# The down projection with its activations standing and its weights moving, in a two-block transformer kernel on one core

## What is computed

```python
def conv_glu_ffn(h, w_gate, w_up, conv_w, conv_b, w_down):
    S = h.shape[1]
    g = h @ w_gate
    gp = jnp.pad(g, ((0, 0), (CONV_WIDTH - 1, 0), (0, 0)))
    gc = conv_b
    for j in range(CONV_WIDTH):
        gc = gc + conv_w[j] * gp[:, j:j + S]
    return (jax.nn.silu(gc) * (h @ w_up)) @ w_down
...
        x = x + jnp.concatenate([y_pool, y_mla, y_mem], axis=-1) @ w_o[l]
        x = x + conv_glu_ffn(rms_norm(x, g_ffn[l]), w_gate[l], w_up[l], conv_w[l], conv_b[l], w_down[l])
```

## Time and profile before

| | |
|---|---|
| median of three runs | 1657.52 us (1654.44 to 1659.46) |
| profiled execution: span | 1662.7 us |
| profiled execution: time beside its span | the profile has none |
| TensorE busy | 1599.2 us, 96% of the span |
| TensorE weight loads | 1454.6 us, 87% |
| VectorE, ScalarE, GpSimd busy | 1163.1, 872.5, 133.3 us |
| mean granted TensorE clock | 0.989 |
| first and last matmul of the down projection start at | 1408.48 and 1658.65 us |

### The profile page before, as it was taken

One profiled execution on the slowest core, in us unless ns is written; L12 is line 12 of the kernel. 1 busy time (PEld: TensorE's weight loads), 2 busy tenths in 40 slices (PEclk: granted clock), 3 DMA queues, 4 the chain that ended last, 5 costly groups with the idle time before them and its releaser, 6 DMA issues.

```text
span 1662.7 us, 26531 instructions
## 1 busy us (share of the span) xinstructions
PE 1599.2 (96%) x10666; PEld 1454.6 (87%) x10666; DVE 1163.1 (70%) x1742; ACT 872.5 (52%) x1360; POOL 133.3 (8%) x151
## 2 busy tenths in 40 slices
PE   6799999988999999898999999999999999999999
PEld 5587789978999999887789888888888888999999
DVE  4777877977668876656677777777777767555553
ACT  5755546667655455554556445444444444444442
POOL 0000000321120220031414000000000000000000
PEclk9999999999999999998999999999999999999999
DMA  8889985533456864342234455555455455555552
GB/s 350 322 311 363 362 319 203 199 99 129 159 197 254 306 240 169 128 153 76 102 127 158 174 200 178 181 200 188 170 199 193 170 195 195 184 180 199 200 185 77
DMA packets 49131, 332.23 MB, mean 200 GB/s; under 512 B 5424, under 2 KB 8880, under 8 KB 9584
## 3 DMA queue, kind: packets, MB, share of 16 engines
q1 hardware_dynamic: 48640, 328.17, 54.1%
q0 software_dynamic: 368, 2.36, 0.4%
HBM read 328.41 MB, written 2.10 MB: 199 GB/s over the span
## 4 chain that ended last, share of the span: by engine, by line
PE 71%; DVE 12%; ACT 8%; issue 4%; DMA 3%; POOL 2%; ACTq 0%; SPq 0%; DVEq 0%; POOLq 0%
PE ps L1085 20%; PE ps L1081 11%; PE ps L1083 10%; PE ps L1082 10%; PE ps L1086 10%; DVE wl L1753 4%; ACT wh L1371 3%; DVE raw L1789 3%; DMA raw<-in_wts 2%; PE ps L1128 2%; PE ps L1129 2%; PE ps L1130 2%; PE ps L1240 1%; PE ps L1207 1%; DVE hA L2173 0%
## 5 line engine op out<-in xcount | busy, mean ns | idle before, releaser
L1753 DVE TENSOR_TENSOR wl<-raw,wh 128x1024 fp32r<-128x1024 f32 x512 | 623.7, 1232 | 356.5 <-ACT wh L1371 355.8
L1371 ACT ACTIVATE wh<-raw 128x1024 fp32r<-128x1024 f32 x512 | 530.5, 1054 | 369.8 <-PE ps L1083 237.0
L1085 PE MATMUL ps<-hA,wh 128*128 128x512 f32 x1408 | 499.2, 400 | 0.0
L1086 PE MATMUL ps<-hA,wl 128*128 128x256 f32 x1408 | 396.2, 281 | 0.0
L1081 PE MATMUL ps<-hB,wh 128*128 128x256 f32 x1280 | 364.5, 285 | 6.5 <-issue 2.4
L1082 PE MATMUL ps<-hB,wh 128*128 128x256 f32 x1280 | 360.4, 282 | 0.0
L1083 PE MATMUL ps<-hB,wl 128*128 128x256 f32 x1280 | 360.3, 282 | 0.0
L1085 PEld LDWEIGHTS ps<-hA,wh 128*128 128x128 f32 x1408 | 265.4, 188 | 66.3
L1086 PEld LDWEIGHTS ps<-hA,wl 128*128 128x128 f32 x1408 | 266.7, 189 | 0.0
L1081 PEld LDWEIGHTS ps<-hB,wh 128*128 128x128 f32 x1280 | 241.9, 189 | 12.6 <-issue 6.7
L1082 PEld LDWEIGHTS ps<-hB,wh 128*128 128x128 f32 x1280 | 242.1, 189 | 0.4 <-issue 0.2
(11 more groups left out here) (271 smaller groups left out, 1569.0 us busy)
## 6 DMA issues: line engine op xcount, KB each, us to landing
raw<-in_wts SPq DMA_DIRECT2D x256, 1024.0 KB, 4.8
raw<-in_ada SPq DMA_DIRECT2D x48, 1024.0 KB, 5.9
work<-in_memN SPq DMA_DIRECT2D x2, 1024.0 KB, 8.4
xs<-in_xN SPq DMA_DIRECT2D x1, 2048.0 KB, 21.3
xs<-in_xT POOLq DMA_DIRECT2D x2, 1024.0 KB, 6.7
out_T<-xs SPq DMA_DIRECT2D x16, 128.0 KB, 2.0
work<-in_cb SPq DMA_DIRECT2D x1, 1024.0 KB, 13.5
wp<-in_dt SPq DMA_DIRECT2D x8, 128.0 KB, 2.3
```

The source lines that it names most:

```text
L1085: e.matmul(ps[bank][:, :], w1, hl, start=first, stop=False)
L1086: i = e.matmul(ps[bank][:, T:2 * T], w2, hl[:, 0:T], start=False, stop=last)
L1371: e.activation(wh[:, h % WS, :], raw[:, n % RAW, part * HALF:(part + 1) * HALF], ACT.Copy).then_inc(s_hi)
L1753: e.tensor_tensor(wl[:, h % WS, :], src, wh[:, h % WS, :].bitcast(F32), ALU.subtract).then_inc(s_lo)
```

## The change

- `w_down` is read K tile by K tile over the full width of 2048, one load for each (44 loads of 1 MB, as before). A half is 1024 columns of one K tile.
- The hidden activations stand (128 x 128: one K tile, 128 tokens), and 512 columns of split weights move. All eight banks hold the result, bank (c, t) for columns 512 c to 512 c + 511 and tokens 128 t to 128 t + 127. K is outermost: each bank is open from the first to the last K tile. `down_half` issues pair 0 (banks 4 to 7) and pair 1 (banks 0 to 3) of a K tile. hid tiles are split into hB once, 44 times.
- The last two K tiles are taken bank by bank (`down_end`): 6 matmuls for each bank, and then VectorE adds it and SP stores it. It waits first for the splits of all four halves.
- x has to be added with tokens as rows. Two side tasks, "xr" 0 and 1, placed after the pairs 1 and 5 of g and u, transpose eight tiles of xs each on TensorE (16 transposes of 128 x 128 into banks 4 to 7), and ScalarE copies the four banks back over the same eight tiles of xs.
- The output has tokens as rows, and 8 stores of 256 KB take the place of 16 of 128 KB.
- hB (and `early` and `E1`, which share its place) is allocated ahead of the constants: it starts at 114,688 and ends at 147,456, where cs begins; work stays where it was.

```diff
+DOWN_BANKS = ((4, 5), (6, 7), (0, 1), (2, 3))
+DOWN_LAST = 2
...
+    xr=dict(turn="p1.8", copy="a2.5"),
...
-    for half in range(2):
-        for u in range(FT // 2):
-            out.append(("s", "w_down_2", [("w_down_2", 2 * u + k, (1024 * half + 128 * j,))
-                                          for k in range(2) for j in range(8)]))
+    for kt in range(FT):
+        out.append(("x", "w_down_2", [("w_down_2", kt, (128 * j,)) for j in range(KT)]))
...
+    def down_half(self, kt, pair):
+        h = self.half
+        self.half += 1
+        self.want(h + self.ahead)
+        self.half_start(h)
+        self.beat("down", h, kt, pair, self.seen("F", kt))
+        self.paced(8)
+        self.half_end(h)
+
+    def down_end(self, kts):
+        h = self.half
+        self.half += 2 * len(kts)
+        self.want(self.half - 1)
+        self.half_start(self.half - 1)
+        self.beat("dend", h, kts)
+        for c in range(4):
+            for t in range(2):
+                self.mids += 1
+                self.end["d", c, t] = "mid", self.mids
+                self.beat("ev", ("d", c, t))
...
+    def turned(i):
+        while ("ms", 1) not in o.done or (i and ("xr", 0) not in o.done):
+            yield
+        yield from stages(("xr", i), ("turn", "copy"))
+
     o.hooks["g", 0] = after_rms(1)
     for j in range(FT):
         o.s_tile(("g", j), "3")
         o.s_tile(("u", j), "3")
         if j < KT:
             o.beat("hs", j)
+        if j in (1, 5):
+            o.add(j // 4 + 1, ("xr", j // 4), turned(j // 4))
+    for c in range(4):
+        for t in range(2):
+            o.take(("d", c, t), DOWN_BANKS[c][t])
     split = KT
-    for part in range(2):
-        for b in range(8):
-            o.take(("d", 8 * part + b), b)
-        for u in range(FT // 2):
-            for kk in range(2):
-                n = part * FT + 2 * u + kk
-                while split < min(n + 12, 2 * FT):
-                    o.beat("hs", split)
-                    split += 1
-                kt = n % FT
-                o.ring_half[n] = o.half + 1
-                o.s_half([(("d", 8 * part + b), b, n, kt == 0, kt == FT - 1) for b in range(8)], "F")
+    for kt in range(FT):
+        while split < min(kt + 12, FT):
+            o.beat("hs", split)
+            split += 1
+        if kt < FT - DOWN_LAST:
+            o.ring_half[kt] = o.half + 2
+            for pair in range(2):
+                o.down_half(kt, pair)
     o.drain()
+    o.down_end(range(FT - DOWN_LAST, FT))
...
         hA = sb("hA", [P, KT, 512], F32R)
         xs = sb("xs", [P, KT, T])
+        early = nc.alloc_sbuf_tensor_at("early", [P, 4096], F32, offset=at[0])
+        E1 = nc.alloc_sbuf_tensor_at("E1", [P, 512], F32, offset=at[0] + 15 * 2048)[:, :]
+        hB = sb("hB", [P, KT, 512], F32R)
         cs = sb("cs", [P, NCST])
         vs = sb("vs", [P, NVEC])
         mk = sb("mk", [P, len(LEVELS), P], U8, 1)
         wp = sb("wp", [P, 4, P])
         ones = sb("ones", [P, P])
         cols = sb("cols", [P, 224])
-        early = nc.alloc_sbuf_tensor_at("early", [P, 4096], F32, offset=at[0])
-        E1 = nc.alloc_sbuf_tensor_at("E1", [P, 512], F32, offset=at[0] + 15 * 2048)[:, :]
-        hB = sb("hB", [P, KT, 512], F32R)
         NW = min((nc.sbuf_top - 64 - at[0]) // 4, 13700)
         work = sb("work", [P, NW])
...
+        def x_rows(c, t):
+            a = 2048 * (c // 2) + 1024 * t + 512 * (c % 2)
+            return flat[:, a:a + 512]
...
-                    j = tile[1]
+                    c, t = tile[1:]
                     e.wait_ge(*after(tile, "dve", "add"))
-                    e.dma_start(out[j * P:(j + 1) * P, :], xs[:, j, :]).then_inc(s_out, 16)
+                    e.dma_start(out[t * P:(t + 1) * P, c * 512:(c + 1) * 512], x_rows(c, t)).then_inc(s_out, 16)
...
-                if first and tile in (("d", 4), ("d", 5), ("d", 6), ("d", 7)):
-                    e.wait_ge(*after(("ms", 1), "dve", "r4"))
...
+            def down_part(h, kt, c, t, first, last):
+                w1, w2 = (w[:, h % WS, c % 2 * 512:c % 2 * 512 + 512] for w in (wh, wl))
+                hi = hB[:, kt % KT, t * P:(t + 1) * P]
+                lo = hB[:, kt % KT, T + t * P:T + (t + 1) * P]
+                po = ps[DOWN_BANKS[c][t]][:, :]
+                e.matmul(po, hi, w1, start=first, stop=False)
+                e.matmul(po, hi, w2, start=False, stop=False)
+                return e.matmul(po, lo, w1, start=False, stop=last)
+
+            def down(h, kt, pair, fresh):
+                e.wait_ge(s_lo, h + 1)
+                if fresh:
+                    e.wait_ge(*moving_ready("F", kt))
+                for c in (2 * pair, 2 * pair + 1):
+                    for t in range(2):
+                        if kt == 0:
+                            was = o.prev["d", c, t]
+                            e.wait_ge(*(after(("xr", 1), "act", "c3") if pair == 0 else bank_clear(was)))
+                        n = down_part(h, kt, c, t, kt == 0, False)
+                n.then_inc(s_half)
+
+            def down_end(h, kts):
+                e.wait_ge(s_lo, h + 2 * len(kts))
+                for kt in kts:
+                    e.wait_ge(*moving_ready("F", kt))
+                for c in range(4):
+                    for t in range(2):
+                        for i, kt in enumerate(kts):
+                            n = down_part(h + 2 * i + c // 2, kt, c, t, False, i == len(kts) - 1)
+                        n.then_inc(s_mid)
+
+            def x_turn(t, k):
+                if k == "turn":
+                    i = t[1]
+                    e.wait_ge(*after(("ms", 1), "dve", "r4"))
+                    if i:
+                        e.wait_ge(*after(("xr", 0), "act", "c3"))
+                    for j in range(8):
+                        e.wait_ge(*after(("o2", 8 * i + j), "dve", "add"))
+                    for r in range(2):
+                        for j in range(8):
+                            n = e.transpose(ps[4 + 2 * r + j // 4][:, j % 4 * P:j % 4 * P + P], xs[:, 8 * i + j, r * P:(r + 1) * P], c_("ident"))
+                    n.then_inc(mark(t, "pe", "turn"))
...
+            def x_turn(t, k):
+                if k == "copy":
+                    e.wait_ge(*after(t, "pe", "turn"))
+                    for r in range(2):
+                        for q in range(2):
+                            e.activation(x_rows(2 * t[1] + q, r), ps[4 + 2 * r + q][:, :], ACT.Copy).then_inc(mark(t, "act", f"c{2 * r + q}"))
...
+                if t[0] == "d":
+                    x = x_rows(*t[1:])
+                    e.wait_ge(*tile_end(t))
+                    e.tensor_tensor(x, x, ps[DOWN_BANKS[t[1]][t[2]]][:, :], ALU.add).then_inc(mark(t, "dve", "add"))
...
-        args.append(nc.dram_tensor("out_T", (D, T), F32, kind="ExternalOutput").ap())
+        args.append(nc.dram_tensor("out_rows", (T, D), F32, kind="ExternalOutput").ap())
```

More of the change, by code:

```diff
@@ L1060, in _ @@
                     ev(b[1])
-            e.wait_ge(s_out, 16 * KT)
+            e.wait_ge(s_out, 16 * 8)
         @block.tensor
@@ L1352, in _ @@
                     s(*b[1:])
+                elif b[0] == "down":
+                    down(*b[1:])
+                elif b[0] == "dend":
+                    down_end(*b[1:])
                 elif b[0] == "m":
```

11 lines of the change are left out of this document (6 added, 5 removed).

## The result

| | before | after |
|---|---|---|
| median, 20 executions each on one chip | 1659.11 us (1653.63 to 1668.17) | 1651.38 us (1645.97 to 1655.6) |
| ratio, 95% interval | | 0.9941 (0.9925 to 0.9956) |
| span of the profiled execution | 1662.7 us | 1650.5 us |
| its time | 1664.5, if its 1.8 us are taken over | 1652.3 us |

The changed kernel is 0.59% faster. The profiles lie 12.2 us apart, where the prediction's terms add up to 3.2.

The account below looks back on a forecast made before the run. TensorE, 96% busy with a stream of matmuls, was taken as the bound. Terms summed to -4.75 us, or -3.2 with the clock's fall, giving 1654.3 us from the 1657.5 median; range 1650.3 to 1660.3.

Parts of the forecast that it names:

- down matmuls: Down projection: 1056 matmuls of 512 columns at 226.7 ns replace 2112 of 256 at 118.5 ns; -11.0 us.
- into the stage: Start of the down projection: its first matmuls go to free banks, so TensorE skips the wait for VectorE's add; -1.7 us.
- two turns: Gate/up stage: two groups of sixteen transposes of x lengthen TensorE's stream, with ScalarE's copies hidden; +3.5 us.
- users of hB: Output projection, latent up-projections and w_o_2: moving from hB's new place costs 119.8 instead of 118.4 ns; +1.9 us.
- last four halves: End of the down stage: TensorE waits for the last weight splits before its last 48 matmuls; +2.7 us.
- clock behind them: After the pause before the last 48 matmuls: TensorE's clock falls, a little likelier than not; +1.6 us, otherwise nothing.
- Rival 2: Down projection: hB as standing operand stays slow at 233.3 ns; 1659.4 us with the clock's fall; chance 0.14.
- rival 4: Down projection: interval follows columns alone, 236.8 ns, so fewer standing-operand changes save nothing; 1665.3 us; chance 0.03.
- rival 3: Gate/up stage: turns of x make ScalarE late for the splits or drop the clock; +8, 1662 us; chance 0.07.
- rival 1: Users of moving hB: its new place doesn't slow them, no +1.9; 1652.4 us with the clock's fall; chance 0.16.
- over to the median: Whole kernel: the difference priced on the 1662.7 us profile was applied to the three-run median, 1657.5 us.
- idle in the gate/up stage: Gate/up stage: idle there would show the prediction wrong, as would a down stage over 248 us.

Follow-up runs that it names:

- e14: Changed kernel with four extra transposes in TensorE's stream behind the ninth pair of gate/up tiles, holding the slow pace after them; 1657.12 us.
- e15: Kernel before with four extra transposes in TensorE's stream behind the ninth pair of gate/up tiles, holding the slow pace after them; 1662.74 us.
- e10: Kernel before with four extra transposes in TensorE's stream behind the third pair of gate/up tiles; 1667.74 us, ratio 1.0038 to the kernel before.
- e4: Changed kernel with hB put back behind the constants, at 125,920; 1661.11 us, ratio 1.0014 to the kernel before.
- e3: Changed kernel with hB and all that lies behind it moved 32 bytes on; 1658.71 us, ratio 0.9999 to the kernel before.
- e11: Changed kernel with the final walk started after three of four splits, and hB viewed 32 bytes on where it moves; 1647.3 us, ratio 0.9919.
- e17: e11 once more, unaltered, on the same chip as e18; 1649.67 us, ratio 0.9907 to the kernel before.
- e12: Changed kernel with 18 interruptions of TensorE's gate/up stream, of 1 to 15 extra transposes each; one execution, 1666.51 us.
- e2: Changed kernel without the two turns of x and their copies, so x is added in the wrong layout; 1651.12 us, ratio 0.9953.
- e5: Changed kernel, nothing altered, measured and profiled a second time; 1651.6 us, ratio 0.9958 to the kernel before.
- e18: Changed kernel, nothing altered, measured and profiled again in a later session; 1649.86 us, ratio 0.9916 to the kernel before.
- e6: Changed kernel with 18 interruptions of TensorE's gate/up stream, of 16, 8, 4 or 1 extra transposes in turn; 1667.74 us.

## Why the prediction was wrong

The forecast was 1654.3 us with "within 0.3%" the likeliest. The direction was right, the size too small. Step by step, in us, profile against profile. "Ahead of hB's users" is the difference up to the first matmul with hB moving; the next row runs from there to the start of the gate/up stage (904.91 and 907.81).

Before:

```profile
522.50 0.36 PE L1081 MATMUL ps<-hB,wh 128*128 128x256 f32 x1
```

After:

```profile
523.59 0.36 PE L1112 MATMUL ps<-hB,wh 128*128 128x256 f32 x1
```

| step | predicted | measured | from |
|---|---|---|---|
| down matmuls | -11.0 | -11.0 | 226.7 ns |
| into the stage | -1.7 | -1.7 | 0.12 instead of 1.79 |
| two turns | +3.5 | +3.5 | 983.92 - 981.82 less one pair: 1.75 each |
| ahead of hB's users | none | +1.1 | 523.59 instead of 522.50 |
| users of hB | +1.9 | +1.8 | 384.22 instead of 382.41 |
| last four halves | +2.7 | +2.6 | 2.86 less one interval |
| clock behind them | +1.6 | +1.5 | 7 intervals in 3.12 us |
| tail | -0.15 | -0.1 | 4.0 instead of 4.05 |
| pace of gate/up | none | -8.1 | 1209 x 6.67 ns |
| pause at 911 | none | -0.4 | 2.02 instead of 2.46 between starts |
| clock behind it | none | -1.5 | rest of the stage's difference |

The measured column sums to -12.3; the profiles' difference is 12.2 (roundings). The mechanisms that the prediction named all came as it said. The row ahead of hB's users is no effect of the change that a run shows: 1.2 us of difference stand at the first matmul behind the memory stage already (84.38 against 83.14 in the earlier trace rows), and the first matmul with hB moving starts anywhere from 519.6 to 525.2 us in the eight profiles with the old code up to there, from 520.9 to 526.4 in the eight with the changed kernel's. Rival 2 fell by 226.7 in the down stage, rival 4 with it; rival 3 by ScalarE's copies and the whole stream around the turns; rival 1 by 120.0 ns for hB moving.

**The step that failed** is the sentence that takes the profiled execution's difference "over to the median", and with it the silent assumption that the stages which the change does not touch keep their time. The profiled execution of the kernel before, its span 5.2 us above the median of three runs and its time 7.0, was one of its upper hump. I noted the 5.2 and didn't ask what they were. What the sum lacked is -8.1 us in the gate/up stage, which ran 1209 pairs at 346.7 instead of 353.3 ns. At equal pace the change is worth 5.6 us by e14 and e15, and 5.4 between the lower hump and the changed kernel; the rest of the 7.7 measured is that the kernel before runs at the slow pace in about 4 of 10 executions (76 of 175), and the changed kernel has only short stretches (198 pairs, 1.3 us) in which it still can, since it was fast behind its second turn in every profile. That the kernel before's share at the slow pace makes the rest is worked out, not shown by a run: I could not hold it at the fast pace, and neither of the two profiles of it unaltered is a fast one. What speaks for it is that e15, held at the slow pace, has no time of twelve below 1660, and e10 none of ten.

**The size at equal pace** was 3.2 predicted, 5.6 measured, with an uncertainty of about 2. By the profile's rows 4.1 are accounted for (12.2 less 8.1), 0.9 more than predicted: the later first use of hB (+1.1), against the shorter pause at 911 and the clock behind it (-1.9). The last two go with hB's place and not with the new down projection: e4, which has that and the old place, has a pause of 2.52 us and the fall behind it, and all four profiles with hB moving from another place than the change's (e3, e4, e11, e17) have 2.5 to 2.9 us and the fall. Why the place shortens the pause stays open. That clock fell behind this pause in all eight profiles with the old down projection, where it is 2.46 to 2.53 us between starts, and in one of the eight that have the changed kernel's code up to that place (2.01 to 2.05 us; e12). The clock behind the pause in the down stage, too, was a draw as the prediction took it: of nine profiles with the same pause of 2.85 us it fell in five (after, e2, e4, e5, e18) and stayed at 1.00 in four (e3, e6, e12, e14).

The Trainium skill's formula for the interval (TensorE: Matmul & The Clock Gate, "Back-to-back issue gap") gives 215.8 ns for 512 columns. The prediction took it for the interval of a stream; the section calls it the gap of an isolated matmul, and has about 131 ns for a stream of 512 columns. The down stage measured 226.7, near the formula and far from 131, and either has one interval for a width where the runs show two or three, by the operand's place. Its remark on transposes ("Part 4: PE-mode transpose") again does not show in groups of sixteen: the window over the second turn, 980 to 985 us, has 1.00 granted.

The prediction's own sign of being wrong, "idle in the gate/up stage", missed the case: beside the wait at 911, which the kernel before has too, there was none. The stream was whole, and faster.

## What to carry to other kernels

- Divide starts by intervals in the stages that a change does not touch as well, and compare them first; a stream without idle time can still run at two paces, and the busy columns show nothing of it.
- When one profile lies some microseconds from the median of the times, look whether the times fall into groups before pricing an edit against it; hold both kernels in one mode (here with four transposes) to compare them.
- Price both sides of a matmul by the place of the operand, standing and moving apart. The place that is best for one can be worse for the other, and two views of one buffer can serve both.

## What the runs showed of the hardware

- A tile standing in hB: 226.7 ns for 512 columns at the change's place (226.7 to 227.2 in the memory stage of all ten such profiles), 233.3 at the old place and 32 bytes on (233.2 to 233.4 in all ten). Moving 256 columns: 120.0, 118.4 and 116.7 ns at these three places.
- The gate/up pair has two paces, 353.3 and 346.7 ns. They differ by 6.67 ns, as 233.3 and 226.7 do. A pace was never seen to change within a stretch, only where other work broke the stream; the same program takes either in different executions. What it hangs on at the break stays open.
- The clock falls or stays behind pauses of the same length at the same place: 2.85 us between starts, five falls in nine profiles.
- Two executions of one program lie microseconds apart long before such a stage: the gate/up stage starts at 902.6 to 910.7 us in the eight profiles with the old code up to there.
